# Two transformer blocks on one core: root mean square applied to rows of scores, and other places and another order for the first expert gathers

## The reference

```python
def peer_ffn(z, ...):                     # z = rmsnorm(h, norm2_g)
    q = (z @ peer_wq)                     # 2048 x 2048, 8 heads, two halves of 128
    s1 = q[:, :, 0] . keys1; s2 = q[:, :, 1] . keys2        # 128 scores each
    v1, i1 = top_k(s1, 16); v2, i2 = top_k(s2, 16)
    cand = v1[:, None] + v2[None, :]      # 256 sums, the best 16 kept
    expert = i1 * 128 + i2                # of those 16
    gate = softmax(top_s)
    act = gelu(peer_u[expert] . z)        # 16 rows of 2048 per token and head
    return sum(gate * act * peer_v[expert])
```

## Time and profile before

| | us |
|---|---|
| median of 3 runs (2513.07 to 2513.39) | 2513.17 |
| the profiled execution | 2512.9 |
| its span, first to last instruction | 2511.1 |
| PE / DVE / ACT / POOL busy | 2161.6 / 1508.2 / 698.6 / 713.5 |
| DMA, HBM over the span | 300 GB/s |

### The profile page before, as it was taken

How to read it: one execution, slowest core, us unless ns; L and a number is a source line. 1 busy time by engine, 2 the same in 40 slices (tenths; PEclk the granted TensorE clock), 3 DMA queues, 4 the chain that set the end, 5 groups by cost and what they waited for, 6 DMA issues and landing times.

```text
span 2511.1 us, 32244 instructions
## 1 busy us (share of the span) xinstructions
PE 2161.6 (86%) x12044; PEld 1605.4 (64%) x12044; DVE 1508.2 (60%) x2144; ACT 698.6 (28%) x1163; POOL 713.5 (28%) x650
## 2 busy tenths in 40 slices
PE   8999999999999999999987668776787668776686
PEld 7999999999999999999943223332333223332232
DVE  5445655555656577857976555655565555655545
ACT  5444544554344344635220000000010000100011
POOL 3000000000001412130574344444444534444342
PEclk9999999999999999999998899888998889988998
DMA  9635454465657555475999999999999999999997
GB/s 273 200 109 152 143 151 150 134 209 177 218 172 241 161 168 162 143 231 152 381 422 421 422 421 422 422 422 422 422 422 421 422 422 422 422 422 422 422 422 299
DMA packets 281388, 755.63 MB, mean 301 GB/s; under 512 B 12032, under 2 KB 213200, under 8 KB 214608
## 3 DMA queue, kind: packets, MB, share of 16 engines
q0 software_dynamic: 74432, 539.07, 51.9%
q1 hardware_dynamic: 206624, 215.28, 27.5%
q10 hardware_dynamic: 240, 0.07, 0.0%
HBM read 752.26 MB, written 2.10 MB: 300 GB/s over the span
## 4 chain that ended last, share of the span: by engine, by line
PE 52%; DMA 36%; DVE 8%; issue 2%; POOL 1%; ACT 1%; ACTq 0%; POOLq 0%; DVEq 0%
PE PS L1756 40%; DMA RZ<-in_peer_u,idxu 19%; DMA RAW<-in_peer_u,idxu 16%; PE PS L2052 7%; DVE RZ L1602 2%; DVE RAW L1602 2%; DVE WL L1091 1%; PE PS L1900 1%; POOL EX L620 1%; DMA EX<-in_peer_v,idxv 1%; PE PS L1827 1%; PE PS L1977 1%; PE PS L1878 1%; DVE SM L1602 1%; PE PS L1888 0%
## 5 line engine op out<-in xcount | busy, mean ns | idle before, releaser
L2052 PE MATMUL PS<-EX,RK 128*128 128x512 f32 x1968 | 907.6, 616 | 315.6 <-ACT RK L1056 188.6
L2052 PEld LDWEIGHTS PS<-EX,RK 128*128 128x128 f32 x1968 | 377.0, 197 | 845.5 <-issue 716.9
L1756 PE MATMUL PS<-XH,WH 128*128 128x256 f32 x2896 | 800.0, 285 | 2.9 <-ACT XH L752 1.8
L1756 PE MATMUL PS<-XH,WL 128*128 128x256 f32 x2896 | 794.0, 283 | 0.0
L1756 PE MATMUL PS<-XL,WH 128*128 128x256 f32 x2896 | 723.5, 283 | 0.0
L1091 DVE TENSOR_TENSOR WL<-RAW,WH 128x1024 fp32r<-128x1024 f32 x380 | 474.2, 1258 | 379.5 <-ACT WH L709 376.0
L1756 PEld LDWEIGHTS PS<-XH,WH 128*128 128x128 f32 x2896 | 555.5, 192 | 4.5 <-issue 2.4
L1756 PEld LDWEIGHTS PS<-XH,WL 128*128 128x128 f32 x2896 | 555.5, 192 | 0.0
L709 ACT ACTIVATE WH<-RAW 128x1024 fp32r<-128x1024 f32 x380 | 400.1, 1059 | 543.4 <-PE PS L1756 534.6
L1756 PEld LDWEIGHTS PS<-XL,WH 128*128 128x128 f32 x2896 | 513.4, 192 | 0.4
L1602 DVE CUSTOM_DVE_ANT_0 RZ<-RZ 128x2048 f32<-128x2048 f32 x126 | 288.8, 2292 | 249.5 <-DMA RZ<-in_peer_u,idxu 249.1
(11 more groups left out here) (344 smaller groups left out, 1349.9 us busy)
## 6 DMA issues: line engine op xcount, KB each, us to landing
RAW<-in_w_in SPq DMA_DIRECT2D x110, 1024.0 KB, 5.2
RAW<-in_w_out SPq DMA_DIRECT2D x32, 1024.0 KB, 5.6
RAW<-in_w_ple_gate SPq DMA_DIRECT2D x16, 1024.0 KB, 5.7
RAW<-in_peer_wq SPq DMA_DIRECT2D x16, 1024.0 KB, 5.7
RAW<-in_w_up_a SPq DMA_DIRECT2D x8, 1024.0 KB, 5.5
RAW<-in_w_up_b SPq DMA_DIRECT2D x8, 1024.0 KB, 5.7
EX<-in_peer_v,idxv POOLq DMA_INDIRECT x252, 27.9
RZ<-in_x SPq DMA_DIRECT2D x2, 1024.0 KB, 6.3
```

Source lines behind the costliest of these rows:

```text
L1756: ins = mm(o[:, t, :], left, right, start=(begins and k == t == m == 0), stop=(ends and k == QUARTER_KT - 1 and m == len(pairs) - 1), skip ...
L2052: ins = mm(bank(4 * (1 - hf) + c), left, right[:, 512 * c:512 * (c + 1)], start=False, stop=True, skip_group_check=True)
```

## The change

- The mean square of GpSimd and PE in "wq" and `rstd` are gone; ACT instead of DVE copies each panel of queries out of its bank, unscaled. The first piece of `choose` multiplies the row of scores by the reciprocal root per token (`rsn`) where it copied before. `token_norm` on DVE is cut into `token_root` and `token_norm`.
- The scores of head 0 are computed after the first quarter of panel 1 instead of the second. The pieces of `choose` and the dots stand at other quarters.
- The 16 U of row 0 have five places, four of them in turns. The four units of `RAW` go to U 0 to 3 of row 1, and these are issued ahead of the eight V of row 0.
- Panels 3 and 5 of "kv" are multiplied with tokens on the rows, and ACT evacuates them into `vall`; PE's transposes and DVE's copies are gone.

```diff
-        EARLY = [SM[:, 0:D], SM[:, D:2 * D], znat[:, 1, :], qhigh, SM[:, 0:D], SM[:, D:2 * D], znat[:, 1, :], qlow,
-                 raw_unit(6, 0), SM[:, 0:D], raw_unit(6, 1), SM[:, D:2 * D], znat[:, 1, :], raw_unit(7, 0), qlow, raw_unit(7, 1)]
-        EARLY_DOTS = {4: 1, 5: 2, 6: 3, 7: 4, 9: 5, 11: 6, 12: 7, 14: 8}
-        EARLY_UNITS = {8: (6, 0), 10: (6, 1), 13: (7, 0), 15: (7, 1)}
-        RAW_DOTS = (9, 11, 14, 16)
+        EARLY = [SM[:, 0:D], SM[:, D:2 * D], znat[:, 1, :], qhigh] + 3 * [SM[:, 0:D], SM[:, D:2 * D], znat[:, 1, :], qlow]
+        EARLY_DOTS = {4: 1, 5: 2, 6: 3, 8: 5, 9: 6, 10: 7, 11: 8, 12: 9, 13: 10, 14: 11, 15: 12}
+        RAW_DOTS, RAW_PANEL, RAW_QUARTERS = (9, 10, 11, 12), (6, 6, 7, 7), (2, 4, 2, 4)
...
-            g.wait_ge(S["lru_y"], 4)
-            line.do(g.memset(acc, 0.0))
-            with g.Fori(0, 2) as i:
-                step = stepper(32, i, 8)
-                for j in range(4):
-                    squares(step, "h2_ready", h2T, i, j)
-            g.sem_inc(S["sum_ready"], 1)
...
-                if k in EARLY_UNITS:
-                    j, u = EARLY_UNITS[k]
-                    g.wait_ge(S["wl_ready"], quarters_before("wq", j) + 2 * u + 2)
                 if k == 7:
                     g.wait_ge(S["sc_done"], 4)
                 gather(peer_u, EARLY[k], u_landed[k % U_SLOTS], idxu, 0, k)
 
+            for k in range(4):
+                g.wait_ge(S["wl_ready"], quarters_before("wq", RAW_PANEL[k]) + RAW_QUARTERS[k])
+                g.wait_ge(S["u_used"], RAW_DOTS[k])
+                gather_u(1, 1, k, reused=False)
             for k in range(V_SLOTS):
                 if k in (0, 4):
                     g.wait_ge(S["w_used"], QUARTERS * PANELS - (2 if k == 0 else 0))
                 gather_v(0, 0, k, reused=False)
-            for k in range(U_AHEAD):
-                if k < 4:
-                    g.wait_ge(S["u_used"], RAW_DOTS[k])
-                if k == 4:
-                    g.wait_ge(S["h2t_done"], 2)
+            g.wait_ge(S["h2t_done"], 2)
+            for k in range(4, U_AHEAD):
+                g.wait_ge(S["u_used"], 9 + k)
                 gather_u(1, 1, k, reused=False)
...
-                line.do(a.activation(kvT[:, j, :, :], tiles2(b), ACT.Copy))
+                if j in VALUES:
+                    typ = VALUES.index(j)
+                    line.do(a.activation(vall[:, :, 2 * typ:2 * typ + 2, :].rearrange("p g s d -> p s g d"),
+                                         tiles2(b).rearrange("p s (g d) -> p s g d", g=GROUPS), ACT.Copy))
+                else:
+                    line.do(a.activation(kvT[:, j, :, :], tiles2(b), ACT.Copy))
...
-                    split_next("wq", j, quarters=(0, 1) if j == 1 else (0, 1, 2))
+                    split_next("wq", j, quarters=(0,) if j == 1 else (0, 1, 2))
                 if 1 <= j <= SCORED:
                     key_scores(j - 1)
                 if j < 7:
-                    split_next("wq", j, quarters=(2, 3) if j == 1 else (3,))
+                    split_next("wq", j, quarters=(1, 2, 3) if j == 1 else (3,))
+                done("wq", j)
+                if j == 4:
+                    a.wait_ge(S["u_used"], 4)
+                b = bank_of("wq", j)
+                a.activation(qp[:, 2 * j:2 * j + 2, :], tiles2(b), ACT.Copy).then_inc(bank_free[b], 1)
                 if j == 0:
-                    a.wait_ge(S["ss_done"], 2)
-                    a.activation(rt[:], bank(3)[:, 0:TOK], ACT.Sqrt, scale=1.0 / D, bias=eps[:, 0:1]).then_inc(S["rt_ready"], 1)
                     token_norm(0)
...
-            def values(typ):
-                v.wait_ge(S["vt_done"], typ + 1)
-                v.tensor_copy(vall[:, :, 2 * typ:2 * typ + 2, :].rearrange("p g s d -> p s g d"),
-                              bank(2 + typ).rearrange("p (s g d) -> p s g d", s=2, g=GROUPS)).then_inc(S["vall_ready"], 1)
-            values(0)
...
-            values(1)
...
-            def token_norm(hf):
+            def token_root(hf):
 
                 v.wait_ge(S["rtn_ready"], 2 + hf + 1)
                 do(v.reciprocal(rsn[:, hf:hf + 1], rtn[:, hf:hf + 1]))
+
+            def token_norm(hf):
...
-                    step(v.tensor_copy(row, scores[:, bass.ds(r, 1)].rearrange("p a s k -> p (a s) k")))
+                    step(v.tensor_scalar(row, scores[:, bass.ds(r, 1)].rearrange("p a s k -> p (a s) k"), rsn[:, hf:hf + 1], None, ALU.mult))
...
-            pieces = {(1, 2): (0, 1), (1, 4): (2, 3, 4), (2, 0): (5,), (2, 1): (6, 7), (2, 2): (8, 9), (2, 3): (10,)}
-            second = {(3, 1): (0, 1, 2, 3), (3, 2): (4,), (3, 3): (5,), (7, 0): (6, 7), (7, 1): (8, 9), (7, 2): (10,)}
-            dots = {(3, 4): 1, (4, 1): 2, (4, 2): 3, (4, 3): 4, (5, 1): 5, (5, 3): 6, (5, 4): 7, (6, 1): 8, (6, 2): 9, (6, 4): 11,
-                    (7, 3): 14, (7, 4): 16}
+            pieces = {(1, 0): (0, 1, 2, 3), (1, 1): (4, 5), (1, 2): (6, 7, 8), (1, 3): (9, 10)}
+            second = {(2, 2): (0, 1), (2, 3): (2, 3), (2, 4): (4,), (3, 0): (5, 6), (5, 1): (7, 8), (5, 2): (9,), (5, 3): (10,)}
+            dots = {(3, 1): 1, (3, 2): 2, (3, 3): 3, (4, 0): 4, (4, 1): 5, (4, 2): 6, (4, 3): 7, (5, 0): 8, (5, 4): 9, (6, 0): 10,
+                    (6, 2): 11, (6, 3): 12, (7, 0): 13, (7, 1): 14, (7, 2): 15, (7, 3): 16}
             dotted = 0
             for j in range(8):
                 for q in range(QUARTERS + 1):
                     if j < 7 and q < QUARTERS:
                         split_next("wq", j, quarters=(q,))
-                    if q == QUARTERS:
-                        if j == 0:
-                            v.wait_ge(S["rt_ready"], 3)
-                            do(v.reciprocal(rstd[:], rt[:]))
-                        b = bank_of("wq", j)
-                        done("wq", j)
-                        if j == 4:
-                            v.wait_ge(S["u_used"], 4)
-                        v.tensor_tensor(qp[:, 2 * j:2 * j + 2, :], tiles2(b), rstd2, ALU.mult).then_inc(bank_free[b], 1)
-
                     if (j, q) == (1, 0):
-                        token_norm(0)
-                    if (j, q) == (1, 2):
+                        token_root(0)
                         v.wait_ge(S["sc_evac"], 1)
                     for piece in pieces.get((j, q), ()):
                         choose(0, 0, 0, piece)
-                    if (j, q) == (2, 3):
+                    if (j, q) == (1, 3):
                         v.tensor_copy(idxu[:, 0, :], expf[:]).then_inc(S["idx_ready"], 1)
                         v.tensor_copy(idxv[:, 0, :], expf[:]).then_inc(S["idx_ready"], 1)
                         v.wait_ge(S["idx_ready"], 2)
-                    if (j, q) == (3, 1):
+                    if (j, q) == (2, 0):
+                        token_norm(0)
+                    if (j, q) == (2, 2):
                         v.wait_ge(S["sc_evac"], 2)
                     for piece in second.get((j, q), ()):
                         choose(1, 1, CHOOSE, piece)
-                    if (j, q) == (7, 2):
+                    if (j, q) == (5, 3):
...
+            token_root(1)
...
-                product("kv", j, middle=compressed if j == 5 else None)
+                product("kv", j, middle=compressed if j == 5 else None, by_tokens=(j in VALUES))
...
-            values(0, 3)
-            values(1, 5)
...
-                if h == 1:
-                    pe.wait_ge(S["rt_ready"], 3)
...
-                product("wq", j, operand="z3" if j == 0 else None, middle=(lambda: key_scores(0)) if j == 1 else None,
+                product("wq", j, operand="z3" if j == 0 else None, second=(lambda: key_scores(0)) if j == 1 else None,
                         third=(lambda: key_scores(j - 1)) if 2 <= j <= SCORED else None)
                 if j == 0:
                     pe.wait_ge(S["keys_evac"], 4)
-                    mean_square(1, 1)
```

More of the change, by code:

```diff
@@ L123 @@
     "xh_ready", "x_ready", "sum_ready", "ss_done", "rt_ready",
-    "kv_evac", "gl_ready", "gates_ready", "vt_done", "vall_ready", "dup_done", "kpad_a", "kpad_v",
+    "kv_evac", "gl_ready", "gates_ready", "vall_ready", "dup_done", "kpad_a", "kpad_v",
     "kab_ready", "hid_done", "hid_tanh", "hid_ready", "kc_done", "kc_ready", "kcdup_done", "kcpad_ready",
@@ L139 @@
 AHEAD = 4
+VALUES = (3, 5)
 V_SLOTS, V_LEAD = 8, 4
@@ L1200, in _ @@
                         .then_inc(S["kpad_v"], 1)
-            values(1)
             v.wait_ge(S["dist_ready"], 1)
             v.wait_ge(S["gates_ready"], 6)
-            v.wait_ge(S["vall_ready"], 3)
+            v.wait_ge(S["vall_ready"], 1)
+            v.wait_ge(S["kv_evac"], 6)
             v.wait_ge(S["kpad_a"], 4)
@@ L1535, in _, with choose @@
             CHOOSE = 28
-            def choose(r, par, before, piece):
+            def choose(r, par, before, piece, hf=0):
                 steps = [(0, 3, 6, 8, 11, 14, 17, 20, 22, 24, 26)[piece]]
@@ L1673, in expert_row @@
                     if k <= 10 and not last:
-                        choose(r + 1, 1 - par, r * CHOOSE + CHOOSE, k)
```

(9 more changed lines are left out.)

## The result

| us | before | after |
|---|---|---|
| median (runs of both on the same chip, 20 each) | 2513.38 (2512.84 to 2516.32) | 2517.23 (2516.41 to 2519.01) |
| the profiled execution | 2512.9 | 2517.89 |
| its span | 2511.1 | 2516.1 |
| PE / DVE / ACT / POOL busy | 2161.6 / 1508.2 / 698.6 / 713.5 | 2165.0 / 1497.7 / 702.4 / 663.8 |

The ratio after to before is 1.0016, 95% interval 1.0010 to 1.0023: 3.85 us slower between the medians, 5.0 us between the two profiled executions. The forecast was 2515.6 us (range 2509.5 to 2519.0) and "same" within 0.2%; the measured step is +0.16%.

What follows compares the result with a forecast made beforehand. The DMA engines, full at 422 GB/s once gathers run without gaps, were taken as the bound. Sixteenth gather +3.4 and front -1.0 gave +2.4: 2515.3 us for the profiled execution, median 0.27 above, 2515.6; range 2509.5 to 2519.

Steps and rivals of the forecast that it cites:

- The premise: Whole kernel: the change can only move the point from which gathers run without gaps, at 2.49 us each.
- the mark: Landing of row 0's sixteenth gather, with 496 following back to back: 1255.8 against 1252.4, 3.4 us later.
- The front: Dense stages before "wq": without transposes and copies of the values, 1.0 us earlier (bounds 0.4 to 1.5).
- The first choice: First choice of experts, in "wq": done earlier, so the first gather goes out 9.5 us earlier.
- DVE's list: DVE's work from 1168.0 to the end of the twelfth dot: 81.1 us, so 1249.1.
- Issue at 1249.2: GpSimd's issue of the sixteenth gather, after the twelfth dot forecast to end at 1249.1.
- the landing: Sixteenth gather from issue to landing: 6.6 us (bounds 5.7 to 7.1), with no weights in flight.
- The head start: First gather 9.5 us earlier, given back because with four places in turns a gather waits for a dot.
- the two idle places forecast: DMA engines idle at about 1201 to 1207 (first dot not yet done) and 1236 to 1251 (second choice).
- Rival (a): Seam: the head start pays, DVE faster than walked or queue never dry, -5.0 us: 2508 us; chance 0.14.
- Rival (b): Seam comes out even, DVE taking 3 us less than walked; only 1.0 us shows: 2512.2 us; chance 0.14.
- Rival (c): Panel 7's third quarter: weights starve behind gathers, deciding from an 18.7 us landing on, +6.2: 2519.4 us; chance 0.14.

Runs made afterwards that it cites:

- e1: The kernel before with only the values of panels 3 and 5 produced by tokens and evacuated by ACT, no transposes or DVE copies: 2512.22 us, ratio 0.9996.
- e6: The changed kernel with two unread one-input sums over 128x2048 added on DVE behind the twelfth dot: 2515.65 us.
- e5: The changed kernel with two unread sums over 128x2048 added on DVE just ahead of the twelfth dot: 2522.04 us.
- e4: The changed kernel with row 1's choice pieces 6 to 10 behind the dots, dots nine to thirteen earlier, V 0 to 7 ahead of row 1's U: 2510.83 us.
- e3: The changed kernel with GpSimd held before its first gather until DVE has split panel 3 in full, about 1193 us: 2521.25 us, ratio 1.0033.
- e7: The changed kernel with row 0's old U places and GpSimd's old order, row 1's last choice pieces behind the dots: 2512.34 us, ratio 0.9995.
- e2: The changed kernel with the first eight V put back ahead of row 1's first four U on GpSimd: 2517.75 us.

## Why the prediction was right

**The premise** held: the seam decides, and bytes moved late are not won back. The sum took the sixteenth gather as the mark, and its move of +4.0 us stands beside a measured +3.85. That these two agree so well is in part luck: the profiled executions moved by 5.0, as the bytes have it (+5.1). What the mark leaves out is that the engines were not at their full rate at once behind it.

**The front** (-1.0): the first product of the main section starts at 159.65 where the earlier trace rows imply 160.63, -0.98. Its parts were off and made up for each other: the doubling of the keys starts at 158.04, which is 0.43 us earlier and not 0.65, and the rest gave 0.55 and not 0.36. As a time it is -1.2 us in e1, not told from zero by its interval.

**The first choice** was due at 1184.5 for the first gather, and it is 1184.51. The table load took the 1.28 us of the earlier trace rows, behind the Square.

**DVE's list**: 81.1 us forecast, 81.7 measured, with the start where it was put (1167.0 after the front's 1.0 us; 1166.98). The scaling took 0.35 to 0.38 us, against 0.29 for the copy: 0.06 and 0.09 more where I had taken 0 out of 0 to 0.13, on two rows 0.15 us in all. Here the trace stands against the Trainium skill (VectorE: DVE Perf Modes, "The perf-mode tier table"), which has both in one class.

**The terms that were mis-sized** are the two behind the dot. "Issue at 1249.2" put 0.1 us between the end of the twelfth dot and GpSimd's issue; it is 1249.54 - 1248.69 = 0.85. The same step, 1211.26 - 1210.40 = 0.86, stood in DVE's and GpSimd's timelines of before, and I had not read it:

```profile
1210.40 0.08 DVE L1602 DVE_READ_ACCUMULATOR2_ANT act<- 128x1 f32 x1
```

```profile
1211.26 1.18 POOL L620 DMA_INDIRECT SM<-in_peer_u,idxu  x1 [10.52 <-DVE act L1602]
```

And the landing was 6.9, not 6.6, still inside its bounds, but not for the reason given: the gather's own issue took 2.25 us beside a dot. In e6, where it took 0.94, the landing was 5.5, below the lower bound of 5.7. The miss adds up: 0.6 (list) + 0.75 (issue) + 0.3 (landing) = 1.65 us, and 2517.23 - 2515.6 = 1.6. For the profiled execution the sum gave 2515.3, which is 2.6 below its 2517.89; the 1.0 us between is what the mark leaves out.

**The head start** was said to be "given back" because DVE's list is too long for it. That is half of the truth. It holds that the twelfth dot decides (e5: +4.8 for 4.4 us of work; e4: 8 us earlier). But e3 shows that the head start was not free to lose: it bought the weights room. The four early gathers were over (1201.0) before the first unit of panel 6 was issued (1202.4). Of the two idle places forecast, the one near 1203 did not appear: loads of weights filled it (share 1.07 at 330 GB/s). The other came where it was foreseen, at 1235, and lasted to 1255.

**Rival (a)**, 2508 us, asked for a twelfth dot 8 us earlier. Its condition was met in e4 (the dot ended at 1240.35, 8.3 us earlier) by another order of the same work, and that gave 2510.8.

**Rival (b)**, 2512.2 us: not met in this kernel; the e7 version comes out there, at 2512.3, but by a wait of 11 us for a unit of weights.

**Rival (c)** did not happen, but its threshold was about right. It was to decide from a landing of 18.7 us on. After the change the two units landed after 18.0 and 16.7 us: ACT stood 6.51 and 3.37 us for them, DVE not at all: ACT's copy of the third quarter was there at 1240.2, and DVE came to it at 1242.0, a margin of 1.8 us. In e4 the unit took 24.1 us, 5.4 more than 18.7, and DVE stood 5.12 for it, in the place where I had put it. In e3 the loads took 23 to 25 us, and DVE stood 3.94 us two units earlier than that, at the third quarter of panel 6.

The 16.5 us of the earlier trace rows were misread: they are not what one unit takes by itself. The unit ahead of it, load L411 of before asked alone at 1212.8, and the last unit of e4, L410 asked alone at 1221.5:

```profile
DMA to landing us min/median/max: 12.8/12.8/12.8
```

```profile
DMA to landing us min/median/max: 24.1/24.1/24.1
```

Timeline of ACT in e4:

```profile
1232.89 2.01 ACT L699 ACTIVATE WH<-RAW 128x1024 fp32r<-128x1024 f32 x2 [6.59 <-DMA RAW<-in_peer_wq]
```

Units land one after the other. Before, the unit issued at 1212.8 landed only at 1225.6, 10.4 us before the 16.5 were over at 1236.0. In e4 ACT waited for the last unit but one until 1232.9, and the last landed 12.7 us later, at 1245.6. So beside gathers a unit comes 10 to 13 us behind the one before it, and what makes its landing long is the queue of units ahead. The prediction's estimate of some 23 us, worked out from the rule of the Trainium skill (DMA: Bandwidth & Descriptors, "Queues, rings and completion order") for one unit with eight gathers passing it, meets e4's 24.1 us by luck: in those 12.7 us the engines moved some 400 GB/s, about 5 MB in all, and that is the unit and four gathers, not eight (an estimate). What the runs show is nearer to the sum of times in the prediction's "against it". At 330 GB/s, the rate where weights moved nearly alone (1200 to 1205 us after the change), a unit takes about 3.2 us of the engines (an estimate); gathers at 2.49 us in every 3.35 leave a quarter of the time, which gives 12.4 us a unit, against the 12.7 of e4.

What spared the changed kernel is its own fault: its second unit landed 5.4 us after the first (1233.8 and 1239.2), because the hole in the gathers, GpSimd's 8.39 us before the thirteenth, let it through. That is read from the two traces, not tested by itself. Holes in the gathers and stands for weights trade against each other here, and a sum that treats them apart gets both wrong.

## What to carry to other kernels

Two streams that share the DMA engines are to be counted as one stretch of bytes: the time follows what is moved by the point from which the engines are full, and work drawn forward in one stream (the head start, the unbroken gathers of e4) shows up as lateness in the other. Of the consumer's list what stands ahead of the last gated issue counts first, so work that nothing waits for yet (row 1's late pieces) belongs behind it; in this kernel that is worth 6.4 us (with V put first, which by itself won nothing in e2), and makes a version 2.6 us faster than before out of a change that was 3.9 us slower. A load's time from issue to landing holds the wait for the loads ahead of it in its queue; read the distance between landings too. From the end of an instruction to the issue of a gather that waits for it, add the 0.8 us that the rows show.

## What the runs showed of the hardware that was not expected

- A gather's issue on GpSimd takes 0.94 us beside one-input work of DVE or none, 1.15 to 1.37 beside short two-input sums, and 1.9 to 3.0 for most of those beside a dot that began before it. The sixteenth gather landed 1.4 us later when its issue was slow (6.9 against 5.5).
- A unit of weights (1 KB packets) lands 10.4 us (before) to 12.7 us (e4) behind the unit before it when gathers (8 KB packets) follow without a hole, and 5.4 us behind it across the hole of the changed kernel. With the units ahead of it in the queue, these took 16.5 to 24.6 us from issue to landing, against 5.7 for the one issued at 1193.2 in the kernel before, just ahead of the first gather (1194.97). Where weights move nearly alone, the engines' share is 1.07 while the rate is 330 GB/s; in the rows of experts it is 1.01 at 422.
- From the row that reads a dot's accumulator to the issue of the gather that waits for it: 0.86 us before, 0.85 after.
